# Activations and vectors laid out by the host with features on partitions, the first norm's squares taken tile by tile, and the output stored as it lies

## What is computed

```python
def rms_norm(x, g):
    return x * rsqrt(mean(x * x, axis=-1) + EPS) * g

def half_ffn(x, i, k):
    h = rms_norm(x, norm_g[i, 2 * k])
    return x + 0.5 * (silu(h @ w_gate[i, k]) * (h @ w_up[i, k])) @ w_down[i, k]

for i in range(2):                       # for the prompt's x and for the samples' x
    x = half_ffn(x, i, 0)
    x = x + mixer[i](rms_norm(x, norm_g[i, 1]))   # gMLP in layer 0, latent attention in layer 1
    x = half_ffn(x, i, 1)
return x_prompt, x_sample, new_mla_prompt, new_mla_sample, new_gmlp_v_sample
```

## Time and profile before

| | us |
|---|---|
| median of 3 runs (2065.03 to 2067.5) | 2067.2 |
| span of the profiled execution, in which all rows below lie | 2065.4 |
| PE busy | 2041.9 (99%) |
| DVE busy | 1609.1 (78%) |
| ACT busy | 1127.1 (55%) |
| POOL busy | 365.1 (18%) |
| PE's first product / the end of its last product | 11.21 / 2058.17 |

### The profile page before, as it was taken

How to read it: one execution, slowest core, us unless ns; L and a number is a source line. 1 busy time by engine, 2 the same in 40 slices (tenths; PEclk the granted TensorE clock), 3 DMA queues, 4 the chain that set the end, 5 groups by cost and what they waited for, 6 DMA issues and landing times.

```text
span 2065.4 us, 44545 instructions
## 1 busy us (share of the span) xinstructions
PE 2041.9 (99%) x16756; PEld 1994.5 (97%) x16756; DVE 1609.1 (78%) x2687; ACT 1127.1 (55%) x1956; POOL 365.1 (18%) x437
## 2 busy tenths in 40 slices
PE   9999999999999999999999999999999999999999
PEld 8999999999999999999999999998789899999998
DVE  7779885437366998998898898669776578989997
ACT  6446554433224665655665555546675556656555
POOL 0011111221011111111111111112232221111111
PEclk9999999999999999999999999999999999999999
DMA  5467783232225777776677777443322126777775
GB/s 171 118 161 178 181 207 105 89 96 73 93 70 125 173 181 179 182 179 158 161 183 177 179 188 176 132 135 89 105 75 80 62 70 161 178 185 176 193 176 130
DMA packets 362556, 295.71 MB, mean 143 GB/s; under 512 B 22103, under 2 KB 327556, under 8 KB 362148
## 3 DMA queue, kind: packets, MB, share of 16 engines
q1 hardware_dynamic: 325498, 227.26, 37.0%
q0 software_dynamic: 36592, 66.07, 19.6%
q10 hardware_dynamic: 314, 0.37, 0.1%
HBM read 224.57 MB, written 2.66 MB: 110 GB/s over the span
## 4 chain that ended last, share of the span: by engine, by line
PE 80%; DMA 7%; DVE 7%; issue 3%; ACT 2%; SPq 1%; DVEq 0%; ACTq 0%
PE main L810 26%; PE side L859 25%; PE main L859 18%; DMA raw<-raw 3%; DMA sums_w<-raw 2%; DMA raw<-in_ffn_w_gate 2%; DVE w_lo L2188 2%; PE side L1413 1%; DMA raw<-in_ffn_w_down 1%; PE main L1162 1%; PE main L1330 1%; PE side L1372 1%; PE side L1250 1%; PE side L1078 1%; PE main L1230 1%
## 5 line engine op out<-in xcount | busy, mean ns | idle before, releaser
L859 PE MATMUL side<-xw_hi,w_hi 128*128 128x260 f32 x1344 | 380.6, 283 | 4.4 <-DVE tmp_in L2337 1.4
L859 PE MATMUL side<-xw_hi,w_lo 128*128 128x260 f32 x1344 | 381.0, 283 | 0.0
L859 PE MATMUL side<-xw_lo,w_hi 128*128 128x260 f32 x1344 | 380.1, 283 | 0.0
L2188 DVE TENSOR_TENSOR w_lo<-raw,w_hi 128x512 fp32r<-128x512 f32 (+2 forms) x472 | 324.1, 687 | 40.1 <-ACT w_hi L1540 20.9
L859 PE MATMUL main<-xw_hi,w_hi 128*128 128x260 f32 x1008 | 286.1, 284 | 0.0
L859 PE MATMUL main<-xw_lo,w_hi 128*128 128x260 f32 x1008 | 284.7, 282 | 0.0
L859 PE MATMUL main<-xw_hi,w_lo 128*128 128x260 f32 x1008 | 284.5, 282 | 0.0
L859 PEld LDWEIGHTS side<-xw_hi,w_hi 128*128 128x128 f32 x1344 | 253.2, 188 | 7.0 <-DVE tmp_in L2337 2.6
L859 PEld LDWEIGHTS side<-xw_hi,w_lo 128*128 128x128 f32 x1344 | 253.1, 188 | 0.0
L859 PEld LDWEIGHTS side<-xw_lo,w_hi 128*128 128x128 f32 x1344 | 252.8, 188 | 0.0
L3132 POOL DMA_DIRECT2D sums_w<-raw x116 | 101.0, 871 | 696.3 <-DMA raw<-in_ffn_w_gate 325.3
(11 more groups left out here) (471 smaller groups left out, 5434.0 us busy)
## 6 DMA issues: line engine op xcount, KB each, us to landing
sums_w<-raw POOLq DMA_DIRECT2D x112, 256.0 KB, 3.3
raw<-raw POOLq DMA_DIRECT2D x112, 256.0 KB, 5.0
raw<-in_ffn_w_gate SPq DMA_DIRECT2D x86, 256.0 KB, 4.6
raw<-in_ffn_w_gate SPq DMA_DIRECT2D x43, 512.0 KB, 5.9
raw<-in_ffn_w_up SPq DMA_DIRECT2D x84, 256.0 KB, 4.7
raw<-in_ffn_w_up SPq DMA_DIRECT2D x42, 512.0 KB, 6.0
raw<-in_gmlp_w_in SPq DMA_DIRECT2D x16, 1024.0 KB, 5.5
raw<-in_ffn_w_down SPq DMA_DIRECT2D x56, 256.0 KB, 4.2
```

Of the source, the lines that this page charges most:

```text
L859: mm = nc.tensor.matmul(into[j], w_tiles(w, weights_at(s, j))[:, k, :], moving[:, k, order[j], :], start=(j in (0, 1) and k == 0 and i == ...
L2188: a = nc.vector.tensor_tensor(dst, src, hi.bitcast(F32), ALU.subtract)
```

## The change

The host lays x out as `x_rows[128, 8, 520]` (both groups of tokens) and all vectors as `vector_cols[128, 103]`, and turns the output back; this lies outside the measured time.

- **Loads.** x goes straight into `x` by five loads in SP's queue (k = 0, 1, 2 to 3, 4 to 5, 6 to 7), the vectors by one load in ACT's queue, followed there by the first quarter of the first gate weights. The other three quarters alternate with x in SP's queue; the up weights in two halves and the constants in one load follow.
- **PE.** All transposes of x, samples and vectors go, and DVE's copies out of PSUM with them. `BUSY` is 10 instead of 12.
- **First norm.** ACT squares the even tiles k (into `square_sum` and `first_squares`), DVE the odd ones. POOL adds the eight tiles up by seven additions in `square_sum`, one behind the other. PE sums over the features by five small matmuls (`sum_tokens`), now behind the second k of the first up tile; the roots are taken from PSUM, and the spread stands behind the fifth k of that tile. DVE makes three of the four rests of the up weights ahead of the reciprocals.
- **ACT.** The dummy activation at the start is a Sqrt instead of a Copy.
- **Output.** `turn_out`, `copy_out` and the copies of the samples go. SP stores tiles of x as they lie: two tiles each behind chunks 0 to 2, then the high half of tile 7, tile 6, and the low half of tile 7.

```diff
-        BUSY = 12
+        BUSY = 10
+        FIRST_X = ((0, 1), (1, 2), (2, 4), (4, 6), (6, KD))
         @block.sync
             load_x(0)
-            load_first(0, 2, first_in[0])
-            for dst, src in vector_sources()[:6]:
-                sp.dma_start(dst, src).then_inc(vectors_in, 16)
             load_x(1)
-            load_first(2, 4, first_in[1])
+            load_first(0, ffn_w_gate[0, 0], 2, 4, first_in[1])
             load_x(2)
-            load_first(4, KD, raw_in[0])
+            load_first(0, ffn_w_gate[0, 0], 4, 6, first_in[2])
             load_x(3)
+            load_first(0, ffn_w_gate[0, 0], 6, KD, raw_in[0])
+            load_x(4)
+            load_first(1, ffn_w_up[0, 0], 0, 4, second_in)
+            sp.dma_start(const[:], table[:, 0:N_CONST]).then_inc(const_in, 16)
+            load_first(1, ffn_w_up[0, 0], 4, KD, raw_in[1])
...
+            for i in range(4):
+                if i < 3:
+                    sp.wait_ge(evac_done, at_end.evac - 12 + 4 * i)
+                else:
+                    sp.wait_ge(evac_done, at_end.evac - 1)
+                sp.wait_ge(row_set, at_end.rows - 3 + i)
+                if i < 3:
+                    store_out(2 * i, 2 * i + 2, slice(0, TOK))
+                else:
+                    store_out(KD - 1, KD, slice(HALF, TOK))
+                    store_out(KD - 2, KD - 1, slice(0, TOK))
+            sp.wait_ge(evac_done, at_end.evac)
+            store_out(KD - 1, KD, slice(0, HALF))
         @block.tensor
                         first_pair()
-                        spread_first()
...
+                                before = {0: lambda: pe.wait_ge(piece_lo, KD), 2: first_token_sums,
+                                          4: lambda: pe.wait_ge(piece_lo, KD + 2), 5: spread_first,
+                                          6: lambda: pe.wait_ge(lo_done, 2)}
...
-                            if final and g == len(at.groups) - 1 and i >= 1:
-                                turn_out((2 * i - 2, 2 * i - 1))
-                        if final and g == len(at.groups) - 1:
-                            turn_out((KD - 2, KD - 1))
         @block.scalar
+            for k in range(0, KD, 2):
+                first_split(k)
+                first_gain(k)
+                first_gain(k + 1)
+                dst = first_squares[:, k, :] if k else square_sum[:]
+                nc.scalar.activation(dst, x[:, k, :], ACT.Square).then_inc(even_squared, 1)
         @block.vector
+            def first_square(k):
+                dve.wait_ge(x_in[x_landed(k)], 16)
+                nc.vector.tensor_tensor(first_squares[:, k, :], x[:, k, :], x[:, k, :], ALU.mult).then_inc(odd_squared, 1)
         @block.gpsimd
+            for k in range(1, KD):
+                if k % 2:
+                    pool.wait_ge(odd_squared, k // 2 + 1)
+                    if k == 1:
+                        pool.wait_ge(even_squared, 1)
+                else:
+                    pool.wait_ge(even_squared, k // 2 + 1)
+                if k > 1:
+                    pool.wait_ge(first_summed, k - 1)
+                nc.gpsimd.tensor_tensor(square_sum[:], square_sum[:], first_squares[:, k, :], ALU.add).then_inc(first_summed, 1)
```

More of the change, by code:

```diff
@@ L866, in token_sums, with first_token_sums @@
                     pe.wait_ge(sum_done, at.sums)
-                    for q in range(QB):
-                        nc.tensor.matmul(side[:, 2, q:q + 1], square_sum[:, q * P:(q + 1) * P], ones[:, 0:1],
-                                         start=True, stop=True)
-                    nc.tensor.matmul(side[0:NS, 2, QB:QB + 1], square_sum[:, SEQ:TOK], ones[:, 0:1],
-                                     start=True, stop=True).then_inc(rms_mm, 1)
+                    sum_tokens(rms_mm)
+                def first_token_sums():
+                    pe.wait_ge(piece_lo, KD + 1)
+                    pe.wait_ge(const_in, 16)
+                    pe.wait_ge(first_summed, KD - 1)
+                    sum_tokens(first_sums)
                 def spread():
@@ L967, in first_pair, with sum_tokens @@
                             mm.then_inc(tile_done, 1)
-                    if k + 3 < KD:
-                        turn_x(k + 3)
             def spread_first():
-                pe.wait_ge(const_in, 16)
                 pe.wait_ge(first_scales, 3)
                 spread_scales(rms_mm)
+            def sum_tokens(signal):
+                for q in range(QB):
+                    nc.tensor.matmul(side[:, 2, q:q + 1], square_sum[:, q * P:(q + 1) * P], ones[:, 0:1],
+                                     start=True, stop=True)
+                nc.tensor.matmul(side[0:NS, 2, QB:QB + 1], square_sum[:, SEQ:TOK], ones[:, 0:1],
+                                 start=True, stop=True).then_inc(signal, 1)
             def spread_scales(signal):
@@ L1691, in down @@
                             norm_tile(at.norm, k, e + k + 1, at.sums - KD)
-            def copy_out(tiles):
-                for k in tiles:
-                    act.wait_ge(out_turned, k + 1)
-                    nc.scalar.activation(y_tok[:, :, k * P:(k + 1) * P], main[:, 1, k % 2, :].rearrange("p (q c) -> p q c", q=QB),
-                                         ACT.Copy).then_inc(out_copied, 1)
             def part_hi(a, b, i):
@@ L3314 @@
     arrays, args = {}, []
-    for name in INPUTS:
-        a = np.ascontiguousarray(inputs[name])
+    for name, a in {**laid_out(inputs), **{name: inputs[name] for name in INPUTS}}.items():
+        a = np.ascontiguousarray(a)
         arrays[f"in_{name}"] = a
@@ L3322 @@
     r = run_bass_kernel_spmd(nc, [arrays], core_ids=[0])
-    return tuple(r.results[0][f"out_{i}"] for i in range(len(OUTPUTS)))
+    y, *rest = (r.results[0][f"out_{i}"] for i in range(len(OUTPUTS)))
+    y = y.transpose(2, 1, 0).reshape(TOK, D)
+    return (np.ascontiguousarray(y[None, :SEQ]), np.ascontiguousarray(y[SEQ:, None]), *rest)
```

249 lines of the change are left out of this document (77 added, 172 removed).

## The result

Over 20 executions of each, the median is 2069.9 us after the change and 2065.2 before: ratio 1.0022, 95% interval 1.0016 to 1.0029. The same comparison on another chip, with 12 executions of the changed kernel, gave 1.0022 again (1.0011 to 1.0033). The change makes the kernel slower by about 4.6 us. That is inside the range (2062 to 2073), but it is not the +0.4 of the sum; by the 0.2% that can be told from no change it is a small loss.

A forecast was written before the change was run, and what follows sets the result against it. PE, busy 2041.9 of 2065.4 us, was taken as the bound, so only its work, waits, start and end count. Head +5.4 and tail −5.0 gave +0.4 on 2067.2: 2067.6, given as 2068, range 2062 to 2073.

The forecast's parts named there:

- the +0.4 of the sum: Whole kernel: head 5.4 us later, tail 5.0 us shorter, together +0.4 us on 2067.2.
- Earlier start: Head: DVE's first rest of x starts at 7.2 (6.5 to 8.2) instead of 10.05, 2.85 us earlier.
- DVE's work in the pair: Head, first pair: eight rests of x, eight of weights and four squares take DVE 10.6 us.
- Turns between DVE and POOL: Head, first pair: seven POOL adds delay DVE 1.17 us each, 8.2 in all (0 to 9.1); last rest ends at 26.0.
- From the last rest to the copy: Head: 7.6 us from DVE's last rest to the copy of the spread scales, at 33.6 instead of 28.25, 5.4 later.
- The stop: Head: PE's stop before the third tile grows from 1.2 to 4.3 us; up tiles end 7.9 us behind the copy.
- The tail: End of kernel: −1.74 from removed transposes and −3.3 behind the last product, in sum −5.0 us (−3.1 to −5.4).
- rival 3: Tail: stores at half speed, so it gives −3.1 and the time is 2069.5; counted within a case of chance 0.48.
- The 1.74: Tail: two groups of eight transposes, 0.87 us each, leave PE's stream between the last products, saving 1.74 us.
- Rival 2: Head: PE's clock falls, 2.7 us on top (2070.3) or 3.9 more (2074.2); taken as 2072, chance 0.27.
- The working for the first pair at the low level: Head: a k takes 2.86 us, so the pair ends at 31.3 instead of 27.4, 3.9 us more, giving 2074.2.
- Adds in DVE's way, clock kept: Head: POOL's adds delay DVE while PE's clock stays up; time 2066.5 to 2070, chance 0.48.

The follow-up runs named there:

- the kernels that compute everything: Changed kernel plus 16 matmuls in the stop: 1.0002 to before; changed kernel with ScalarE squares, VectorE additions, 16 warm-up and 12 stop matmuls: 0.9963, 0.9973 to before.
- the version above without idle matmuls: Changed kernel with ScalarE squaring all tiles, VectorE adding, spread two k earlier, 10 warm-up matmuls, none in the stop: ratio 0.9984 to the kernel before.
- the version with all stretches filled: Changed kernel with ScalarE squares, VectorE additions, spread two k earlier, 16 warm-up matmuls, 12 in the stop: ratios 0.9963 and 0.9973 to the kernel before.

## Why the prediction was right or wrong

- **Earlier start: right.** DVE started at 6.97; 7.2 was predicted.
- **DVE's work in the pair: right.** 10.6 predicted, 10.6 measured without POOL.
- **Turns between DVE and POOL: right in mechanism, a little too large.** 8.2 predicted, 7.5 measured (1.07 for each addition instead of 1.17). The two meetings of the earlier trace rows were enough to price a row of seven additions. By the exclusive lock that the Trainium skill states ("SBUF — State Buffer", section "Who interferes with whom") the same sum would have been 9.1; the trace shows a little overlap left.
- **From the last rest to the copy: right.** 7.6 predicted, 7.7 measured (25.05 to 32.78). The copy was 4.5 late, 5.4 predicted: 0.2 from the start and 0.7 from the additions.
- **The stop: right.** 4.3 predicted, 4.08 measured, and from the cause that was worked out, some 8 us of products behind the copy: it is 4.10 without the additions too.
- **The tail: 5.0 predicted, 4.6 in the trace, 3.7 alone.** The part behind the last product was right (3.85 predicted, 3.5 measured), and rival 3, stores at half speed, is out. The 1.74 rested on the step that failed: "since the chain is PE alone there" held for the profiled execution of before; once the transposes go, the wait for the next chunk's weights can take their place. Over the ten traces with the new output the two chunks gain 1.8 at most (all of the 1.74, as in the second trace of the changed kernel) and lose 2.6 at worst; in the first trace of the changed kernel they gain 0.9.
- **The clock: the term that was left out of the sum.** Rival 2 was given 0.27. Its sign, products some 0.24 apart behind the stop, came in both traces of the changed kernel (0.217), with a granted clock of 0.50. By the Trainium skill's rule ("TensorE: Matmul & The Clock Gate", Part 1) the low level is the default; the fall that the rows of before did not show is now in the rows. The fall does not take the place of the likeliest case, as the prediction put it, but adds to it: the rival's smaller sum, 2.7 on top, is of that kind, with 5.5 us at half pace where 3.5 were seen, worth 1.5 in the trace, while the whole stop is worth 4.1 in the time. The working for the first pair at the low level (3.9) did not come about: PE ran at 0.217 until 14 us only, and by the end of the pair DVE was the pace, so that nothing of it came through. "Adds in DVE's way, clock kept" and "clock falls" were written as two cases, but the fall does not hang on the additions: without them the stop and the half pace are there too.
- **The base.** 2067.2 was the median of three executions; with 20 it is 2065.2. The predicted 2068 comes within 2 of 2069.9 since this 2 and the missing 4 go against each other; that nearness is luck.

## What to carry to other kernels

An addition that is given to an idle GpSimd isn't free where VectorE works on SBUF at the same time: one meeting of the two in a trace gives its price, and the price times the count belongs in the sum. Where other engines take up a result while TensorE goes on with other products, compare the two lengths: here some 8 us of products against a chain of 12.2 made a stop of 4 us, which was followed by some 3.5 us at half pace in all five traces that have it. Matmuls that nobody reads, put into such a stop and ahead of the first product, were worth 2 to 4 us in the kernels that compute everything. And a wait that a removed step had covered can come out: the last two chunks, the same 16.2 us in three traces with transposes, took 14.4 to 18.8 without them.

## What was not expected of the hardware

- A stop of 1.2 us (before) or 2.66 us (the version above without idle matmuls) left TensorE at its upper level; one of 4.08 us was followed by a granted clock of 0.50, and the level rose again at 48.5, 3.5 us after the first product. But waits of 2.44 and 2.63 us in the last chunks were followed by 0.50 too, and one of 2.34 in the kernel with the additions on VectorE was not: from the length of a stop alone these traces do not tell the fall.
- The granted clock is shown as 1.00 at the start of the changed kernel's trace while products come 0.217 apart, until 14 us. The window:

```profile
8.00:14.00 6.00, 5.88 (x27) 5.88 (x28) 6.00 (x9) 6.00 (x11) 4.09 (x2) 1.00 1.04 385
```

and in the timeline of PE

```profile
9.58 0.64 PE L935 MATMUL main<-start_hi,w_hi 128*128 128x260 f32 x2
...
14.57 0.40 PE L935 MATMUL main<-start_hi,w_hi 128*128 128x260 f32 x2
```

In this trace one reads the level there from the pace, not from that column. In five other traces with ten warm-up matmuls the column itself shows 0.50 at 10 us.
- The spread between executions goes along with the idle stretches: 12 executions without additions, with idle stretches of PE, lie between 2058 and 2072, and 19 of the version with all stretches filled between 2057 and 2066. That the clock makes the whole of that difference is not shown.
